# Compression's first layer with the token spans stationary in two column halves, fourteen gate tiles by half-size products, and all token sums on GpSimd

## The chip, the cores and the metric

One core of one Trainium2 chip runs the whole program. The metric is the device time of one execution in microseconds (us); less is better. Engines are named as in the profile: PE (TensorE matmuls), PEld (its weight loads), DVE (VectorE), ACT (ScalarE), POOL (GpSimd), SP (SyncE, which issues the transfers). All data are float32, which the profile records as two PE instructions for each matmul.

## What is computed

A decoder trunk of two equal layers on 512 tokens of 1024 channels. Each layer:

```
h = rmsnorm(x);  z = h @ W_in
q, kc, vc, ks, vs, kw, vw, nsa_g, u, g_a, g_s = split(z)
a = NSA(...)        # compressed + selected blocks + sliding window
s = S5(u)           # grouped complex-diagonal state space, then GLU
x = x + (sigmoid(g_a) * (a @ proj_nsa) + sigmoid(g_s) * (s @ proj_s5)) @ W_out
x = x + HierMoE(rmsnorm(x))     # top-1 group, top-2 of its experts
```

The first layer of the compression, on which the change works, is this; each of the 31 blocks takes 32 tokens of 64 channels, and two neighbours share 16 tokens:

```
def compress(t, pos_emb, w1, w2):           # once for keys, once for values
    blocks = heads(t, Hkv)[:, :, blk_idx] + pos_emb      # 2 heads x 31 blocks x 32 x 64
    flat = blocks.reshape(B, Hkv, n_cmp, CMP_BLOCK * dh)
    return jax.nn.gelu(flat @ w1) @ w2                   # w1: 2048 x 128
```

## The kernel before

**Stages.** A layer runs in three stages: the projections and the mixer's inputs, then attention with the state space, then the experts. PE sets the pace of the first two; in the third the weights of the experts stream through SP's queue (489.25 MB are read from memory in the whole program). The loads of the experts are issued as the arena's places come free of the mixer, so that whatever moves the mixer's end moves the experts. The second layer is the same code and runs the same order.

**The two merge gates as fill.** g_a and g_s make 16 tiles of 128 channels x 512 tokens. They are needed only at the merge, so PE computes them in small pieces between other work, by `fill(cost)` (L918). The unit is one matmul 128x256 wide. `FILL` lists the pieces in order. `PLAIN` pairs of tiles (2 pairs, so 4 tiles) are computed directly, as matmuls 128x512 (L935). The other twelve tiles (`FAST` = 6 pairs) are computed by Strassen-Winograd: seven products of half size for each pair (L916, 128x256), of sums of weights (`weight_sum`, L667, POOL) and sums of tokens (`token_sums`, L1984, DVE: t1 to t4, 128x1024 each). Two products go to the two halves of one bank; ACT copies the bank out (`evac_fill`, L1496) and POOL adds it to the gate tiles (`half_sums`, L634; L632). `ORDER` is the order of the seven products, and `FILL_AHEAD` is the work that is placed ahead of the scores of attention: 80 units.

**Around the first layer of the compression.** PE's order is written out by hand: the transposes tq(t) and tk(t) of the normalised queries and keys (L996, L1001), `hid` (L972), the output steps of the state space `s5y` (L1060, eight steps of 12 matmuls, four of them each on 32 columns of the array), with `cmp` (second layer of the compression, L892) and `tkc` (transpose of the compressed keys, L1004) between them, then the scores (L1074, L1084). In `hid` the weights `w1[:, c, m, :]` (c: keys or values, m: one of 16 token pairs) are stationary, 128 columns, and the tokens `k2` move, 93 columns wide at a stride of 8: 62 blocks of the two heads and 31 columns of the position embedding, whose column gives the bias of the gelu. There are 16 x 2 matmuls, in two banks, and after three of four m a `fill(2)`, 12 in all.

**DVE and POOL there.** DVE normalises queries and keys of tile t in `norm_qk(t)` (L1862 to L1880), runs `chunk_scan` (L1961 to L1982), whose end raises `states_ready` for s5y, and then the four token sums (L1997). `chunk_scan` begins when PE has transposed the last keys, ("tk", 3). POOL fills the position columns of k2 (L625) early, then waits for ("tk", 3), clears two tiles (L628) and makes the first four weight sums (L679) before the sums of the products' results.

**Chunks of weights.** The columns of W_in arrive through four places, numbered by `RING_AT`. A place is loaded again when `last_use` says it was read; the last chunks are those of the projections ahead of the merge.

Of the kernel before, what the change touches and what calls it, by code (L numbers as in the profile page):

```python
# [20 lines left out]
ALU = mybir.AluOpType  # L21
# [3 lines left out]
P = 128  # L25
D = 1024
S = 512
# [44 lines left out]
PLAIN = 2  # L72
FAST = 8 - PLAIN
C_FAST = 5 + PLAIN
RING_AT = [0, 1, 2] + [3, 3] + [3, 2] + [0, 2] * (FAST // 2) + [1, 0, 2]


def chunk_before(c):

    if c == C_FAST + FAST:  # L80
        return c - 2
    return max((i for i in range(c) if RING_AT[i] == RING_AT[c]), default=None)
# [6 lines left out]
GROUPS += [("hid", 0), ("hid", 1), ("cmp", 0), ("cmp", 1), ("tkc", 0)]  # L89
# [7 lines left out]
ORDER = (1, 6, 2, 7, 4, 5, 3)  # L97
PRODUCTS = [(j, n) for j in range(FAST) for n in ORDER]
FILL = [("gate", i) for i in GATES[:2 * PLAIN]] + [("fast", g) for g in range(14)]
for m in range(4):  # L100
    FILL += [("z", m), ("fast", 14 + m)]
FILL += [("fast", g) for g in range(18, len(PRODUCTS) // 2)]
# [4 lines left out]
def fill_cost(g):  # L107

    return 2 * KD if g[0] == "gate" else 4 if g[0] == "z" else KD


FILLED = 2 * PLAIN + 2
# [69 lines left out]
def trunk(nc, a, out):  # L182
    with ExitStack() as ctx:
# [78 lines left out]
        k2 = view(76, 2, KVH + 1, S // 2)  # L262
# [15 lines left out]
        w2 = view(98, 2, DH)  # L278
        us5 = view(110, NST, S5J)
# [14 lines left out]
        rtmp = spare[:, 2 * D:2 * D + 384].rearrange("p (i g d) -> p i g d", i=4, g=12)  # L294
        fast_p = [spare[:, 2432 + S * i:2432 + S * i + S] for i in range(2)]
# [127 lines left out]
        cpos_zero = sem("cpos_zero")  # L423
        cpos_ready = sem("cpos_ready")
        kv_zero = sem("kv_zero")
# [63 lines left out]
        def last_use(c):  # L489

            if c < 3:
                return pj_done, GIDX[("tok", c + 2, NT - 1)] + 1
# [18 lines left out]
        def fast_tokens():  # L511
# [3 lines left out]
                        t1=raw[:, :, 0:256], t2=raw[:, :, 256:512], t3=hT[:, LOW, LATE], t4=t4)  # L515
# [62 lines left out]
        def _(pool):  # L578
# [40 lines left out]
            with pool.Fori(0, DEPTH) as l:  # L619
                for i in range(2):  # L620
                    pool.memset(k2[:, i, KVH, :], 0.0).then_inc(cpos_zero, 1)
                pool.wait_ge(cpos_zero, 2)
                pool.wait_ge(mix_in, N_MIX_IN)
                for i in range(2):
                    pool.tensor_copy(k2[:, i, KVH, 0:CSTR], cpos[:, i, :]).then_inc(cpos_ready, 1)  # L625
                pool.wait_ge(pj_done, GIDX[("tk", NT - 1)] + 1)
                for y in (vcs, kcT):
                    pool.memset(y, 0.0).then_inc(kv_zero, 1)  # L628
# [51 lines left out]

                for n in range(1, 5):
                    weight_sum(0, n)
                for g in range(len(PRODUCTS) // 2):
# [188 lines left out]
        def _(pe):  # L872
# [26 lines left out]
            def fast_product(j, n, k):  # L899
# [6 lines left out]
                elif n == 7 and k == 0:  # L906
                    pe.wait_ge(h_sums, 4)
                    pe.wait_ge(w_sums, 4 * j + 3)
# [4 lines left out]
                dst, w, h = bank[:, FB, HALVES[half]], fast_weights(j)[a][:, k, :], fast_tokens()[b][:, k]  # L913
                if n == 4:
                    dst = dst.rearrange("p (b d) -> p b d", b=2)
                return pe.matmul(dst, w, h, start=(half == 0 and k == 0), stop=(half == 1 and k == KD // 2 - 1))  # L916
# [26 lines left out]
            def group(g, tap=None):  # L943
# [20 lines left out]
                elif kind == "hid":  # L964
# [3 lines left out]
                    pe.wait_ge(cpos_ready, 2)  # L968
                    n = KVH + 1
                    for m in range(CSTR):  # L970
                        for c in range(2):
                            r = pe.matmul(bank[:, (i + c) % NBANK, 0:n * NCMP].rearrange("p (h c) -> p h c", h=n),  # L972
                                          w1[:, c, m, :], k2[:, c, :, m:m + CSTR // 2 * (NCMP - 1) + 1:CSTR // 2],
                                          start=(m == 0), stop=(m == CSTR - 1))
                            if m == CSTR - 1 and c == 0:
                                r.then_inc(pj_done, 1)
                        if m % 4 < 3:
                            fill(2)
# [1345 lines left out]
```

## Time and profile before

| what | value |
|---|---|
| device time, median of 3 | 1830.31 us (1829.23 to 1834.97) |
| the profiled execution | 1832.97 us, span 1831.3 us |
| span of one layer | 907.85 us from L1961 of the first to that of the second |
| PE busy | 1664.1 us, 91% |
| DVE, ACT, POOL busy | 580.3, 411.5, 201.1 us |
| granted TensorE clock, mean | 0.973 of full |

Times inside the program are us from the span's start. The rows below are of the first layer unless they say otherwise.

### The profile page before, as it was taken

Reading aid. Unit: us, or ns where it says so; the run is one execution under the profiler, and the core shown is the slowest. Engines: PE = TensorE matmul, PEld = TensorE weight load, DVE = VectorE, ACT = ScalarE, POOL = GpSimd, SP = SyncE. Lnnn points to the kernel's source line nnn. Section 1 sums busy time; section 2 is a strip of 40 time slices with the busy share of each in tenths; the row PEclk is TensorE's granted clock in tenths of the full one; section 3 lists DMA queues with packets and bytes.
Section 4 is the critical chain, followed back from the end, with each engine's and each line's share of the span. In section 5 each row is a group of like instructions: output and inputs, shape, how many; then the busy total and the mean of one; then the engine's idle time right before and its main releaser. Section 6 shows DMA issues by size and latency. Waiting matters only on the chain. (4 is left out here: it accounts for less than half of the span.)

```text
span 1831.3 us, 22306 instructions
## 1 busy us (share of the span) xinstructions
PE 1664.1 (91%) x7754; PEld 878.8 (48%) x7754; DVE 580.3 (32%) x1686; ACT 411.5 (22%) x1003; POOL 201.1 (11%) x289
## 2 busy tenths in 40 slices
PE   8999999999998778788899999999999987878888
PEld 6667766454443333333377677554544433323333
DVE  4875356334000000000278744563340000000003
ACT  3323555011111111111123254540111111110101
POOL 1012421000100100000000134210001100000000
PEclk9999999999999989999999999999999999998999
DMA  6631101564999999999947111026569999999998
GB/s 171 142 106 47 47 24 47 207 253 177 409 426 428 427 425 426 427 427 428 390 113 195 52 47 47 24 54 237 227 242 412 426 427 427 425 428 427 427 427 345
DMA packets 121906, 496.44 MB, mean 271 GB/s; under 512 B 42036, under 2 KB 78900, under 8 KB 94160
## 3 DMA queue, kind: packets, MB, share of 16 engines
q1 hardware_dynamic: 109584, 472.75, 65.2%
q0 software_dynamic: 8928, 16.52, 2.4%
q10 hardware_dynamic: 3296, 5.84, 0.8%
q8 instruction: 64, 1.05, 0.2%
q14 instruction: 34, 0.28, 0.0%
HBM read 489.25 MB, written 30.47 MB: 284 GB/s over the span
## 5 line engine op out<-in xcount | busy, mean ns | idle before, releaser
L1262 PE MATMUL bank<-arena 128*64 128x512 f32 x2176 | 694.3, 622 | 88.5 <-DMA arena<-in_expert_up 31.3
L1262 PEld LDWEIGHTS bank<-arena 128*64 128x64 f32 x2176 | 229.8, 143 | 352.0 <-issue 351.8
L2224 DVE SCALAR_TENSOR_TENSOR arena<-bank,halves,arena 128x512 f32<-128x512 f32 x32 | 24.0, 751 | 815.0 <-PE bank L1262 815.0
L1262 PE MATMUL bank<-spare_slot,arena 128*64 128x512 f32 x320 | 138.1, 630 | 29.9 <-ACT arena L1664 9.1
L1262 PE MATMUL bank<-h,arena 128*64 128x512 f32 x320 | 140.5, 615 | 26.9 <-DMA arena<-in_expert_gate 11.9
L892 PE MATMUL bank<-arena,hT 128*128 128x256 f32 (+1 forms) x512 | 119.5, 390 | 3.3 <-DMA arena<-in_w_in 2.5
L1262 PE MATMUL bank<-hT,arena 128*64 128x512 f32 x256 | 119.4, 622 | 0.0
L1155 PE MATMUL bank<-arena,hT 128*128 128x512 f32 x256 | 115.0, 597 | 0.0
L892 PEld LDWEIGHTS bank<-arena,hT 128*128 128x128 f32 x512 | 96.7, 192 | 19.9 <-issue 2.7
L1662 ACT ACT_TABLE_LOAD x32 | 41.1, 1283 | 264.8 <-PE bank L1262 264.8
L916 PE MATMUL bank<-hT,arena 128*128 128x256 f32 x384 | 97.0, 387 | 0.0
L1262 PEld LDWEIGHTS bank<-h,arena 128*64 128x64 f32 x320 | 42.1, 141 | 110.3 <-issue 110.3
L1262 PEld LDWEIGHTS bank<-spare_slot,arena 128*64 128x64 f32 x320 | 41.6, 145 | 110.2 <-issue 110.2
L1664 ACT ACTIVATE arena<-bank 128x512 f32<-128x512 f32 x32 | 19.1, 597 | 307.9 <-PE bank L1299 307.9
L1547 ACT ACTIVATE arena<-bank,nbias 128x32 f32<-128x32 f32 (+4 forms) x192 | 83.3, 447 | 6.5 <-DVE nbias L2031 6.4
L892 PE MATMUL bank<-arena 128*128 128x512 f32 (+1 forms) x216 | 84.1, 551 | 0.0
L916 PEld LDWEIGHTS bank<-hT,arena 128*128 128x128 f32 x384 | 68.5, 191 | 14.7 <-issue 7.8
L916 PE MATMUL bank<-h,arena 128*128 128x256 f32 x288 | 72.0, 386 | 0.0
L1155 PEld LDWEIGHTS bank<-arena,hT 128*128 128x128 f32 x256 | 46.6, 190 | 49.4 <-issue 49.4
L2031 DVE TENSOR_REDUCE nbias<-bank 128x1 f32<-128x128 f32 (+3 forms) x128 | 54.8, 483 | 46.2 <-PE bank L1086 46.2
L935 PE MATMUL bank<-hT,arena 128*128 128x512 f32 x128 | 66.5, 601 | 1.0 <-ACT arena L1505 0.9
L679 POOL TENSOR_TENSOR arena<-arena 128x512 f32<-128x512 f32 x48 | 61.5, 1282 | 0.6
(377 smaller groups left out, 1948.5 us busy)
## 6 DMA issues: line engine op xcount, KB each, us to landing
arena<-in_expert_up SPq DMA_DIRECT2D x48, 2048.0 KB, 38.1
arena<-in_expert_gate SPq DMA_DIRECT2D x44, 2048.0 KB, 34.1
arena<-in_expert_down SPq DMA_DIRECT2D x44, 2048.0 KB, 38.9
arena<-in_w_in SPq DMA_DIRECT2D x26, 1024.0 KB, 6.1
spare_slot<-in_expert_gate SPq DMA_DIRECT2D x8, 2048.0 KB
h<-in_expert_gate SPq DMA_DIRECT2D x8, 2048.0 KB
hT<-in_expert_up SPq DMA_DIRECT2D x8, 2048.0 KB, 40.8
spare_slot<-in_expert_down SPq DMA_DIRECT2D x8, 2048.0 KB
```

Of the source, the lines that this page charges most:

```text
L679: pool.tensor_tensor(out=w[out_], in0=w[x1], in1=w[x2], op=op).then_inc(w_sums, 1)
L892: r = pe.matmul(dst, w, m, start=(i == 0), stop=(i == len(pairs) - 1))
L916: return pe.matmul(dst, w, h, start=(half == 0 and k == 0), stop=(half == 1 and k == KD // 2 - 1))
L935: r = pe.matmul(bank[:, FB, :], lhs, rhs, start=(k == 0), stop=(k == n - 1))
L1155: r = pe.matmul(bank[:, c, :], mergedT[:, k, P * t:P * t + P], w_o[:, c, k, :], start=(k == 0), stop=(k == KD - 1))
L1262: r = pe.matmul(dst[CAP * e:CAP * e + CAP, :], moving[:, k, CAP * e:CAP * e + CAP], w, start=(k == 0), stop=(k == n - 1))
L1547: act.activation(p, s, ACT.Exp, scale=-1.0, bias=nbias[:, n % 2, i:i + 1], accum_out=rsum[:, n % 2, i:i + 1])\
L1662: act.activation(hid, bank[:, 2, :], ACT.Silu, scale=slot_root).then_inc(silu_done, 1)
L1664: act.activation(actT.rearrange("p a b -> p (a b)"), bank[:, 6, :], ACT.Copy).then_inc(at_ready, 1)
L2031: dve.tensor_reduce(nbias[:, n % 2, i:i + 1], bank[:, i, 0:nk], AX.X, ALU.min).then_inc(max_ready, 1)
L2224: STT(hid, bank[:, 3, :], slot_root, hid, ALU.mult, ALU.mult).then_inc(act_ready, 1)
```

## The change

Per layer, five things.

1. **Gates.** `PLAIN` 2 to 1 and `FAST` 6 to 7: fourteen tiles by products, two directly. The order of the seven products changes, 49 products make 25 groups (the last with one product), and attention takes 164 units of fill where it took 168. `RING_AT` and `last_use` follow.
2. **First layer of the compression.** The tokens are stationary now: `windows` takes 63 blocks (62, and one of no use between the heads) of k2 at a stride of 8, and w1, 128 columns wide, moves. Keys go to the columns and partitions 0 to 62 of one bank, values to 64 to 126. Ahead of them two matmuls put the position term there: `ones` (64 columns) against `hid_pos`. The output is token by channel, so that after the gelu (one ACT instruction, 128x128) a transpose `th` on PE and a copy on ACT bring it round for `cmp`. A `fill(2)` follows each of the 16 m.
3. **Position term.** `hid_pos` is computed by DVE between `norm_qk(3)` and `chunk_scan`: w1 of each m times the position's value, summed over m, 2 + 30 instructions of 128x128. PE's `hid` waits for all of them (`cpos_ready`).
4. **Token sums.** t3, t2, t4, t1 go from DVE to POOL (t3, t2, t1 with 128x1024, t4 in two halves of 512), with t2 in a place of its own. The first four weight sums come ahead of them and wait for the last token projection, not for ("tk", 3). The sums for the fourth group wait for `states_ready`.
5. **s5y** has its `fill(2)` in four of eight steps only, and `th` stands behind its first step.

```diff
-PLAIN = 2
+PLAIN = 1
-RING_AT = [0, 1, 2] + [3, 3] + [3, 2] + [0, 2] * (FAST // 2) + [1, 0, 2]
+RING_AT = [0, 1, 2] + [3, 3] + [3] + [0, 2] * (FAST // 2) + [0] + [2, 3, 0]
-ORDER = (1, 6, 2, 7, 4, 5, 3)
+ORDER = (1, 2, 6, 7, 4, 5, 3)
...
-FILLED = 2 * PLAIN + 2
+FILLED = 2 * PLAIN + 6
...
+                pool.wait_ge(pj_done, GIDX[("tok", 5, NT - 1)] + 1)
                 for n in range(1, 5):
                     weight_sum(0, n)
-                for g in range(len(PRODUCTS) // 2):
+                b = fast_tokens()
+                halves = lambda y: y.rearrange("p (a k) s -> p a k s", a=2)
+                pool.wait_ge(fill_done, 2 * PLAIN)
+                pool.tensor_tensor(out=b["t3"], in0=b["b22"], in1=b["b12"], op=ALU.subtract).then_inc(h_sums, 1)
+                pool.wait_ge(h_sums, 1)
+                pool.tensor_tensor(out=tok_t2, in0=halves(b["t3"]), in1=halves(b["b11"]), op=ALU.add).then_inc(h_sums, 1)
+                pool.wait_ge(pj_done, GIDX[("tk", NT - 1)] + 1)
...
+                for g in range((len(PRODUCTS) + 1) // 2):
+                    if g == 3:
+                        pool.wait_ge(states_ready, 2)
...
-                    pe.wait_ge(cpos_ready, 2)
-                    n = KVH + 1
+                    pe.wait_ge(ones_ready, 1)
+                    pe.wait_ge(cpos_ready, 2 * CSTR)
+                    for c in range(2):
+                        pe.matmul(b[DH * c:DH * c + DH, 0:P], ones, hid_pos[:, c, :], start=True, stop=False)
+                    n = KVH * (NCMP + 1) - 1
+                    windows = k2.rearrange("p c h t -> p c (h t)")
                     for m in range(CSTR):
                         for c in range(2):
...
+                            r = pe.matmul(b[DH * c:DH * c + n, 0:P],
+                                          windows[:, c, m:m + CSTR // 2 * (n - 1) + 1:CSTR // 2], w1[:, c, m, :],
+                                          start=False, stop=(m == CSTR - 1))
...
+                elif kind == "th":
+                    pe.wait_ge(pj_evac, GIDX[("hid", 0)] + 1)
+                    r = pe.transpose(b[:, 0:P], ghid[:, :], ident[:, :])
...
-                            if part == 0:
+                            if part == 0 and k == 0:
                                 fill(2)
...
                 evac(("hid", 0))
-                evac(("hid", 1))
+                evac_fill(6)
+                evac(("th", 0))
...
-                        TT(b[out_], x1, x2, ALU.subtract).then_inc(h_sums, 1)
-
+                dve.wait_ge(mix_in, N_MIX_IN)
+                for m in range(CSTR):
+                    for i in range(2):
+                        w, c = w1[:, i, m, :], cpos[:, i, m:m + 1]
+                        if m:
+                            dve.wait_ge(cpos_ready, 2 * (m - 1) + i + 1)
+                            r = STT(hid_pos[:, i, :], w, c, hid_pos[:, i, :], ALU.mult, ALU.add)
+                        else:
+                            r = TS(hid_pos[:, i, :], w, c, None, ALU.mult)
+                        r.then_inc(cpos_ready, 1)
                 dve.wait_ge(pj_done, GIDX[("tk", NT - 1)] + 1)
                 chunk_scan()
-                token_sums(1, 2)
-                token_sums(4, 3)
```

The next listings show the order of instructions on an engine, one row for each run of like ones (arena, hT and h are the large buffers; bank is PSUM).

PE at the beginning of the first layer of the compression, before:

```order
L996 MATMUL bank<-ident,arena 128x128 x4
L1001 MATMUL bank<-ident,h 128x128 x2
L935 MATMUL bank<-hT,arena 128x512
L972 MATMUL bank<-arena 128x93 x2
L935 MATMUL bank<-hT,arena 128x512
```

and after, where L938 is the half-size product:

```order
L1023 MATMUL bank<-ident,arena 128x128 x4
L1028 MATMUL bank<-ident,h 128x128 x2
L938 MATMUL bank<-hT,arena 128x256 x2
L993 MATMUL bank<-arena 64x128 x2
L998 MATMUL bank<-arena 63x128 x2
L938 MATMUL bank<-arena 128x256 x2
```

The wide direct gate matmuls are gone from between the pairs, and each pair stands between half-size products; the two position matmuls (L993) lead.

PE at its end, before:

```order
L972 MATMUL bank<-arena 128x93 x2
L1060 MATMUL bank<-arena,spare_slot 32x128 x4
L916 MATMUL bank<-hT,arena 128x256 x2
L1060 MATMUL bank<-arena 32x128 x8
L892 MATMUL bank<-arena 31x64 x6
```

and after:

```order
L998 MATMUL bank<-arena 63x128 x2
L938 MATMUL bank<-arena 128x256 x2
L1087 MATMUL bank<-arena,spare_slot 32x128 x4
L938 MATMUL bank<-hT,arena 128x256 x2
L1087 MATMUL bank<-arena 32x128 x8
L1007 MATMUL bank<-ident,arena 128x128
L1087 MATMUL bank<-arena,spare_slot 32x128 x4
```

One step of s5y stands ahead of the transpose `th` (L1007), and another between it and `cmp`.

POOL ahead of the sums of the results, before (with the semaphores it waits for):

```order
L625 COPY arena<-cpos 128x16
L628 MEMSET arena 128x256 [waits pj_done]
L628 MEMSET arena 128x64
L679 TENSOR_TENSOR arena<-arena 128x512 [waits ring_in0]
L679 TENSOR_TENSOR arena<-arena 128x512 [waits w_sums]
L679 TENSOR_TENSOR arena<-arena 128x4x128
```

and after:

```order
L679 TENSOR_TENSOR arena<-arena 128x512 [waits w_sums]
L687 TENSOR_TENSOR hT<-hT 128x4x256 [waits fill_done]
L689 TENSOR_TENSOR arena<-hT 128x2x512 [waits h_sums]
L695 TENSOR_TENSOR h<-hT,arena 128x2x2x128 [waits h_sums,pj_done]
L697 TENSOR_TENSOR h<-hT,arena 128x4x256
L699 MEMSET arena 128x256
```

DVE in the same place, before:

```order
L1865 TENSOR_TENSOR h<-spare_slot 128x2x2x8
L1866 TENSOR_TENSOR h<-spare_slot 128x2x2x8
L1961 TENSOR_TENSOR arena<-bank,arena 128x1024
L1962 TENSOR_TENSOR arena<-bank,arena 128x1024
L1963 TENSOR_TENSOR arena<-bank,arena 128x1024
```

and after:

```order
L1894 TENSOR_TENSOR h<-spare_slot 128x2x2x8
L1895 TENSOR_TENSOR h<-spare_slot 128x2x2x8
L2021 TENSOR_SCALAR arena<-arena,cpos 128x128 x2
L2019 SCALAR_TENSOR_TENSOR arena<-arena,cpos 128x128 x30
L1990 TENSOR_TENSOR arena<-bank,arena 128x1024
```

The 32 instructions of the position term stand between the last normalisation and the scan on DVE, beside POOL's token sums of five instructions.

## Rows read from the trace of the kernel before

**Rows 1.** The page: the mean GB/s of transfers in 40 equal slices.

```profile
GB/s 171 142 106 47 47 24 47 207 253 177 409 426 428 427 425 426 427 427 428 390 113 195 52 47 47 24 54 237 227 242 412 426 427 427 425 428 427 427 427 345
```

**Rows 2.** Windows: stretch; its length, busy us (instructions) of each engine; clock, DMA.

```profile
130.00:152.30 22.30, 22.21 (x90) 15.27 (x88) 22.04 (x31) 1.64 (x5) 5.26 (x6) 1.00 0.00 1
```

**Rows 3.** Waits of PE from 100 to 330: total us, times, longest.

```profile
PE bank L1114 <- DVE arena L2057: 1.6, 8, 0.2
...
PE bank L935 <- ACT arena L1505: 0.5, 1, 0.5
```

**Rows 4.** Timeline of PE at hid: start, length, instructions (two records a matmul).

```profile
130.73 0.90 PE L972 MATMUL bank<-arena 128*128 128x93 f32 x4
...
132.32 0.84 PE L972 MATMUL bank<-arena 128*128 128x93 f32 x4
132.98 1.04 PE L935 MATMUL bank<-hT,arena 128*128 128x512 f32 x2
...
152.31 0.43 PE L1060 MATMUL bank<-arena,spare_slot 128*32 128x128 f32 x8
```

**Rows 5.** Timeline of PE: half-size products alone, and one matmul pair on 64 columns.

```profile
168.66 3.67 PE L916 MATMUL bank<-h,arena 128*128 128x256 f32 x16
172.26 0.38 PE L1084 MATMUL bank<-arena 64*128 64x128 f32 x2
...
179.55 0.65 PE L1114 MATMUL bank<-arena,h 128*64 128x256 f32 x4
180.13 0.92 PE L916 MATMUL bank<-h,arena 128*128 128x256 f32 x3
```

**Rows 6.** Timeline of PE: one step of s5y with its fill, and the next.

```profile
162.44 0.40 PE L1060 MATMUL bank<-arena,spare_slot 128*32 128x128 f32 x8
162.77 1.13 PE L916 MATMUL bank<-hT,arena 128*128 128x256 f32 x4
163.83 0.64 PE L1060 MATMUL bank<-arena 128*32 128x128 f32 x16
164.29 0.40 PE L1060 MATMUL bank<-arena,spare_slot 128*32 128x128 f32 x8
```

**Rows 7.** Timeline of ACT: second direct gate copied out; table load of hid's gelu.

```profile
124.33 0.60 ACT L1505 ACTIVATE arena<-bank 128x512 f32<-128x512 f32 x1 [5.67 <-PE bank L935]
...
152.42 1.28 ACT L1469 ACT_TABLE_LOAD   x1
```

**Rows 8.** Timeline of DVE: 128x128 pieces; the scan's beginning, idle time ahead in brackets.

```profile
90.72 0.29 DVE L1797 TENSOR_TENSOR arena<-arena,turnv 128x128 f32<-128x128 f32 x1
90.93 0.28 DVE L1798 TENSOR_TENSOR arena<-arena,turnv 128x128 f32<-128x128 f32 x1
...
129.83 1.22 DVE L1961 TENSOR_TENSOR arena<-bank,arena 128x1024 f32<-128x1024 f32 x1 [8.61 <-PE bank L1001]
...
134.48 2.02 DVE L1965 TENSOR_TENSOR arena<-arena 128x1024 f32<-128x1024 f32 x1
136.42 1.21 DVE L1966 TENSOR_TENSOR arena<-arena 128x1024 f32<-128x1024 f32 x1
```

**Rows 9.** Timeline of POOL: weight sums, later one sum of results.

```profile
130.22 5.20 POOL L679 TENSOR_TENSOR arena<-arena 128x512 f32<-128x512 f32 x4
...
247.33 0.76 POOL L632 TENSOR_TENSOR arena<-spare_slot 128x256 f32<-128x256 f32 x1 [5.92 <-ACT spare_slot L1503]
248.05 1.38 POOL L679 TENSOR_TENSOR arena<-arena 128x512 f32<-128x512 f32 x1
```

**Rows 10.** Timeline of DVE: the same four instructions, beside POOL and without it.

```profile
246.76 2.89 DVE L2050 TENSOR_SCALAR arena<-arena,rscale 128x384 f32<-128x384 f32 x4
...
254.24 1.41 DVE L2050 TENSOR_SCALAR arena<-arena,rscale 128x384 f32<-128x384 f32 x4
```

**Rows 11.** Windows around an idle stretch of PE among the experts.

```profile
678.00:680.30 2.30, 0.00 (x0) 0.03 (x1) 0.00 (x0) 0.00 (x0) 0.00 (x0) 0.50 1.04 440
680.30:684.80 4.50, 4.50 (x12) 1.56 (x14) 0.00 (x0) 0.00 (x0) 0.00 (x0) 0.50 0.99 419
```

More of the change, by code:

```diff
@@ L88 @@
 GROUPS += [x for t in range(NT) for x in (("tq", t), ("tk", t))]
-GROUPS += [("hid", 0), ("hid", 1), ("cmp", 0), ("cmp", 1), ("tkc", 0)]
+GROUPS += [("hid", 0), ("th", 0), ("cmp", 0), ("cmp", 1), ("tkc", 0)]
 GIDX = {g: i for i, g in enumerate(GROUPS)}
@@ L278, in trunk @@
         w2 = view(98, 2, DH)
+        ghid = view(98.5, P)
+        hid_pos = view(99, 2, P)
+        ones = view(80, DH)
         us5 = view(110, NST, S5J)
@@ L619, in _ @@
             with pool.Fori(0, DEPTH) as l:
[L620 to L628, printed above, removed]
+                pool.memset(ones, 1.0).then_inc(ones_ready, 1)
                 def add(out_, x1, x2):
@@ L679, in weight_sum @@
                     pool.tensor_tensor(out=w[out_], in0=w[x1], in1=w[x2], op=op).then_inc(w_sums, 1)
+                pool.wait_ge(pj_done, GIDX[("tok", 5, NT - 1)] + 1)
                 for n in range(1, 5):
                     weight_sum(0, n)
-                for g in range(len(PRODUCTS) // 2):
+                b = fast_tokens()
[5 more added lines that the diff above has]
+                pool.wait_ge(pj_done, GIDX[("tk", NT - 1)] + 1)
+                pool.wait_ge(h_sums, 2)
+                for i in range(2):
+                    two = slice(2 * i, 2 * i + 2)
+                    blocks = lambda y: y.rearrange("p k (b d) -> p k b d", b=2)
+                    pool.tensor_tensor(out=b["t4"][:, two], in0=blocks(b["b21"][:, two]), in1=blocks(tok_t2[:, i]),
+                                       op=ALU.subtract).then_inc(h_sums, 1)
+                pool.tensor_tensor(out=halves(b["t1"]), in0=halves(b["b22"]), in1=tok_t2, op=ALU.subtract).then_inc(h_sums, 1)
+                for y in (vcs, kcT):
+                    pool.memset(y, 0.0).then_inc(kv_zero, 1)
+                for g in range((len(PRODUCTS) + 1) // 2):
+                    if g == 3:
+                        pool.wait_ge(states_ready, 2)
                     group_sums(g)
@@ L912, in fast_product @@
                 half = product_at(j, n) % 2
-                dst, w, h = bank[:, FB, HALVES[half]], fast_weights(j)[a][:, k, :], fast_tokens()[b][:, k]
+                dst, w, h = bank[:, FB, HALVES[half]], fast_weights(j)[a][:, k, :], (tok_t2[:, k // 2, k % 2] if b == "t2" else fast_tokens()[b][:, k])
                 if n == 4:
                     dst = dst.rearrange("p (b d) -> p b d", b=2)
-                return pe.matmul(dst, w, h, start=(half == 0 and k == 0), stop=(half == 1 and k == KD // 2 - 1))
+                return pe.matmul(dst, w, h, start=(half == 0 and k == 0), stop=((half == 1 or (j, n) == PRODUCTS[-1]) and k == KD // 2 - 1))
             def fill(cost):
@@ L1383, in _ @@
                 s5_step(("s5y", 0, 1))
+                group(("th", 0))
+                s5_step(("s5y", 1, 2))
                 group(("cmp", 0))
                 group(("cmp", 1))
-                s5_step(("s5y", 1, S5L))
+                s5_step(("s5y", 2, S5L))
                 group(("tkc", 0))
@@ L1618, in _ @@
                     evac(("tk", t))
[L1619 removed]
+                for i in range(2, 6):
                     evac_fill(i)
                 evac(("hid", 0))
[L1622 removed]
+                evac_fill(6)
+                evac(("th", 0))
                 evac(("cmp", 0))
@@ L1625, in _ @@
                 qk_roots(NT)
-                table_of(ACT.Gelu_apprx_tanh, 3)
+                table_of(ACT.Gelu_apprx_tanh, 1)
                 act.wait_ge(states_ready, 2)
-                evac_fill(4)
+                evac_fill(7)
                 gelus(0)
                 evac(("tkc", 0))
-                evac_fill(5)
                 gelus(1)
```

70 lines of the change are left out of this document (30 added, 40 removed).

## The prediction

> **What bounds the kernel now.** I read the mean transfer rate over the 40 slices first: after the first quarter of each layer it stays near 427 GB/s for some ten slices, the experts [rows 1]. The experts take their places in memory as the mixer leaves them, so a microsecond won or lost in the mixer is one at the end, and the second layer repeats the first. Then the window of the first compression layer: PE is busy 22.21 of 22.30 us and so is DVE (22.04), POOL 5.26 [rows 2]. PE's waits over the whole of attention are three groups, 1.6, 1.5 and 0.5 us, two of them shown [rows 3]. So the mixer is PE's own work, and what counts is, per layer: PE time removed, and any place where PE now waits for another engine.
>
> **PE time, per layer.**
>
> *Fill units.* A direct tile costs 16 units, a product 4, and 16 more units belong to the state space's gates: 4 x 16 + 42 x 4 + 16 = 248 before, 2 x 16 + 49 x 4 + 16 = 244 after. A unit is 0.43 us: 16 records, 8 matmuls, lie between 168.66 and 172.26, 3.60 us with one change of shape [rows 5]. So -4 x 0.43 = **-1.7**.
>
> *The first layer itself.* Two matmuls (four records) take 132.98 - 132.32 = 0.66 us [rows 4]; 16 pairs are 10.6, and with the changes between them the 21.58 us from 130.73 to 152.31 [rows 4] less 12 fills of two units (24 x 0.43 = 10.3) leave about 10.9. The new pair exists in no row. Low bound: both halves work side by side, so a pair costs one matmul of 128 columns, half of 0.43, and the two changes of shape to the fill and back: in a step of s5y the fill of 0.86 takes 163.83 - 162.77 = 1.06 [rows 6], so 0.20; together 0.42. High bound: the two 64-column matmuls of 256 columns took 0.58 [rows 5], and 0.20 on top is 0.78, if what fills these 0.58 is not the columns but the loads of two stationary blocks, which are as many here. They stand between fills in both cases; I take the middle, 0.61. The two position matmuls move 128 columns like one pair and have only the change behind them open: 0.5. 16 x 0.61 + 0.5 = 10.3: **-0.6** (bounds -3.7 and +2.1).
>
> *Fill out of s5y.* A step with its fill takes 164.29 - 162.44 = 1.85 [rows 6]. Without it there are 24 records at the 0.46 for 16 that 163.83 to 164.29 show, 0.69. The fill's own 0.86 moves to hid, so each step saves 0.30: four steps **-1.2**.
>
> *Transpose th.* 0.22 (half a unit) and two changes of shape: **+0.4**.
>
> Sum of PE work: **-3.1**. The array's rule of the Trainium skill speaks for more: TensorEngine Tiling (Array Packing), section "Performance Considerations", gives swapping the operands with two column tiles when the moving side is at most 64 wide, twice the work at a time. By it this term would be -4.9 (5.5 + 0.5 for 10.9), not -0.6. Its section "Key Properties" takes part back, since a change of tiling mode drains the engine, and every pair here stands between two such changes.
>
> **The wait for the position term.** Before, DVE is idle for 8.61 us ahead of 129.83 [rows 8]; hid_pos is placed there, and PE can't start hid (130.73 before) until the last of the 32 is done. Alone they would fit: 128x128 pieces start 0.21 us apart (90.72, 90.93) [rows 8], 32 x 0.21 = 6.7, ready at 121.2 + 6.7 = 127.9. But POOL is at work in the same stretch now. What the trace shows of the two together: L1965 adds two inputs from the large buffer while POOL's four weight sums run (130.22 to 135.42) and takes 2.02; L1966 after them, the same size, takes 1.21 [rows 8, 9]. L1961, with one input in PSUM, took 1.22 beside them. And four L2050 take 2.89 beside two POOL instructions (0.76 and 1.38) against 1.41 without [rows 9, 10]. The 1.48 more are the two POOL instructions less one DVE instruction of 0.33 each: (0.76 - 0.33) + (1.38 - 0.33) = 1.48. So DVE gets about one instruction for each of POOL's. The scaled sums of hid_pos have two inputs from the large buffers, as L1965 has.
>
> The Trainium skill states this as an exclusive lock (SBUF — State Buffer, section "Who interferes with whom"): a DVE instruction with two SBUF inputs contends with a GpSimd instruction that reads SBUF, and who issues first keeps the port for the whole instruction. The trace agrees with its 2.02 against 1.21; no row shows it for a scaled sum, and the page names only `tensor_tensor` for it.
>
> Now the schedule. Weight sums (4 x 1.27 or so: 5.20 for four [rows 9]) start when the last token projection is out, near 106, beside norm_qk(2); they push the statistics of tile 3 and so the end of norm_qk(3) from 121.2 to about 122.4. POOL's t3 starts when the second direct gate has been computed, 124.3 [rows 7]; until then DVE does 9 of 32. POOL: 256 elements take about 0.73, 512 1.27, so 1024 about 2.36; t3, t2 to 129.1, a wait for ("tk", 3) until 129.8, then 2 x 1.27 + 2.36 to 135.0. DVE gets one instruction beside each of the five and three in the gap, 17 done at 135; the other 15 take 3.2, last one at 138.2. PE starts hid at about 138.3, not 130.7: **+7.6** (bounds 5.5, if DVE gets two for one, and 9). Queued behind on DVE are the scan's 20.3 us (129.83 to 150.1), which end near 158 and with six to nine POOL sums beside them 160 to 164; PE's hid takes 24.1 with its 16 fills and ends at 162.4. So s5y waits 0 to 1.7 for the states: **+0.4**.
>
> *Clock.* PE idle for 7.6 us. Among the experts PE has no instruction from 678.00 to 680.30, the granted clock there is 0.50, which is 1.2 of 2.4 GHz, and it stays so for another 4.5 us of work [rows 11], worth 2.2. Here, with a longer idle stretch, part of it may pass before work begins: **+1.7** (0.5 to 2.3).
>
> *The chain behind hid.* Gelu waits for its table, 1.28 [rows 7], then th, its copy on ACT, cmp, the key norm, tkc. Before, PE's steps with fill covered it. Now ACT has evac_fill(6) ahead of the copy of th, and that waits for POOL's sums of the fourth group, which start at `states_ready`; and PE has four fills fewer to do in between. ACT's copy and POOL's pair of sums are 0.6 and 1.5, of which one step of s5y (1.85) covers the most. I take **+1.2** for th and **+0.6** for tkc (0 to 3 together).
>
> Costs nothing: the third chunk of the rings (its load ends some 20 us ahead of the merge), the later half-sums (POOL idle more than half of attention), four token sums off DVE (DVE is not waited for there).
>
> **Sum.** -3.1 + 7.6 + 0.4 + 1.7 + 1.8 = +8.4 a layer, +16.8 for two. The profiled execution would take 1832.97 + 16.8 = 1849.8; it stood 2.7 above the median, and against the median of 1830.3 that is **1847**.
>
> **Rivals.** What a measurement can tell from no change is about 0.3%, 5.5 us.
> - *A: scaled sums don't contend.* hid_pos ends at 128.5 and hid starts as before. For it: 8.61 us idle hold 6.7 of work. Against it: 2.02 and 2.89 [rows 8, 10]. -3.1 + 1.8 = -1.3 a layer: 1827.7.
> - *B: as A, and the chain behind hid is hidden too* (s5y steps cover 1.85 each). -3.1 a layer: 1824. This is the case on the other side, faster than before; it decides as soon as the position term is out before 130.7 and th finds its copy ready.
> - *C: DVE keeps the port and POOL waits.* hid_pos is done at 129, t3 and t2 at 134, and PE stands at its first product with t2, 131.7, for 2.3 us: -1.3 + 2.3 = +1.0 a layer: 1832.
> - *D: pairs cost 0.78* with weight loads in the open, the change doesn't bring the side-by-side work it is written for: +2.7 a layer on the forecast: 1852.
> - *E: pairs at 0.34*, half of the present 0.68 (10.9 / 16), with no change of shape felt: 16 x 0.27 = -4.3 a layer on the forecast: 1838. For it: s5y's four-fold tiling has 16 records in 0.46 [rows 6]; against it: the 0.20 of the same rows. It is what the Trainium skill's rule on swapped operands would give.
>
> **How the numbers follow.** Forecast 0.50, A 0.14, B 0.08, C 0.08, D 0.12, E 0.08. Faster by over 0.3% (below 1824.8): B and a third of A, 0.12. Within: the rest of A, C and a little of the forecast's low end, 0.19. Slower: 0.69. The range goes from A's low side, 1826, to the forecast with the high ends of pair and states, 1855; B and the tail above are left out.
>
> **What would show it.** In the profile after: hid's first matmul at 138 with an idle stretch on PE ahead released by DVE; single 128x128 scaled sums on DVE of 1.2 to 2.4 us while POOL's five sums run and 0.29 else; clock 0.50 behind it; a pair of hid 0.6 after a fill; 1.5 between fills. Wrong it would be if hid starts at 131 (A or B), or if PE's first wait is for token sums (C).

## The result

The changed kernel takes 1842.87 us (median of six, 1840.28 to 1846.01), the kernel before 1829.77 (six, 1828.06 to 1834.97): ratio 1.0071, interval 1.0061 to 1.0081. It is slower by 13.1 us, where 16.8 were forecast. The sign and the range held, but the wait that costs most is not the one the forecast was built on.

### The profile page after: what moved, and what is told of

The parts are those of the page before. It is cut to its first block and busy times, and to the rows that moved or that the text cites. A ratio compares the mean times of both kernels' runs of the same rounds, so it can differ in the third digit from the quotient of the medians.

```text
span 1841.4 us, 22540 instructions
## 1 busy us (share of the span) xinstructions
PE 1656.9 (90%) x7812; PEld 875.1 (48%) x7812; DVE 612.9 (33%) x1742; ACT 415.6 (23%) x1007; POOL 259.4 (14%) x315
## 5 line engine op out<-in xcount | busy, mean ns | idle before, releaser
L1289 PE MATMUL bank<-spare_slot,arena 128*64 128x512 f32 x320 | 132.2, 610 | 30.9 <-ACT arena L1693 9.1
L938 PE MATMUL bank<-hT,arena 128*128 128x256 f32 x448 | 114.1, 388 | 1.7 <-ACT spare_slot L1532 1.6
L679 POOL TENSOR_TENSOR arena<-arena 128x512 f32<-128x512 f32 x56 | 73.9, 1321 | 173.7 <-PE bank L911 172.5
L938 PEld LDWEIGHTS bank<-hT,arena 128*128 128x128 f32 x448 | 79.5, 190 | 18.8 <-issue 6.1
L732 POOL COPY slot_tok<-table 128x1 int32 x28 | 5.1, 183 | 499.4 <-DVE arena L2234 499.4
L632 POOL TENSOR_TENSOR arena<-arena,spare_slot 128x256 f32<-128x256 f32 x70 | 51.2, 747 | 133.8 <-ACT spare_slot L1532 119.7
```

The lines of the kernel that those rows point to most:

```text
L632: return pool.tensor_tensor(out=out_, in0=x1, in1=x2, op=ALU.add)
L679: pool.tensor_tensor(out=w[out_], in0=w[x1], in1=w[x2], op=op).then_inc(w_sums, 1)
L1289: r = pe.matmul(dst[CAP * e:CAP * e + CAP, :], moving[:, k, CAP * e:CAP * e + CAP], w, start=(k == 0), stop=(k == n - 1))
```

## The profile after

PE's waits from 100 to 340, changed kernel (columns as in [rows 3]):

```profile
PE bank L938 <- issue: 3.9, 1, 3.9
PE bank L1141 <- DVE arena L2079: 1.6, 8, 0.2
PE bank L1129 <- DVE arena L2072: 1.4, 4, 0.4
PE bank L938 <- ACT spare_slot L1532: 1.1, 4, 0.3
PE bank L1031 <- DVEq L2030: 0.6, 1, 0.6
...
```

The second line is the first of [rows 3]; the third stood before at 1.5 us, in the part of [rows 3] that is not printed. New are the first (3.9 us), the fourth (ACT copies the products' bank) and the fifth (tkc). There is no wait for the position term. "issue" names no releaser; the timelines of PE, DVE and POOL say which it is. PE:

```profile
129.55 0.44 PE L993 MATMUL bank<-arena 128*64 128x128 f32 x4
129.79 0.43 PE L998 MATMUL bank<-arena 128*63 128x128 f32 x4
134.10 1.10 PE L938 MATMUL bank<-arena 128*128 128x256 f32 x4 [3.88 <-issue]
135.13 0.71 PE L998 MATMUL bank<-arena 128*63 128x128 f32 x4
135.77 2.08 PE L938 MATMUL bank<-arena 128*128 128x256 f32 x4
...
144.76 1.13 PE L938 MATMUL bank<-h,arena 128*128 128x256 f32 x4
145.82 0.51 PE L998 MATMUL bank<-arena 128*63 128x128 f32 x4
146.26 1.13 PE L938 MATMUL bank<-h,arena 128*128 128x256 f32 x4
...
159.96 0.43 PE L1087 MATMUL bank<-arena,spare_slot 128*32 128x128 f32 x8
```

DVE, then POOL:

```profile
121.40 7.96 DVE L2019 SCALAR_TENSOR_TENSOR arena<-arena,cpos 128x128 f32<-128x128 f32 x30
129.28 1.21 DVE L1990 TENSOR_TENSOR arena<-bank,arena 128x1024 f32<-128x1024 f32 x1
```

```profile
123.22 8.36 POOL L687 TENSOR_TENSOR hT<-hT 128x1024 f32<-128x1024 f32 x1 [12.60 <-PE bank L957]
131.66 2.35 POOL L689 TENSOR_TENSOR arena<-hT 128x1024 f32<-128x1024 f32 x1
134.15 4.34 POOL L695 TENSOR_TENSOR h<-hT,arena 128x512 f32<-128x512 f32 x2
```

PE begins the position matmuls at 129.55, on time: hid_pos is out at 129.3. It then has nothing to do until 134.10, where the first product that reads t2 begins (L938 from the arena). t2 (L689) ends at 134.01. It is late because t3 (L687) is recorded with 8.36 us, where t2, a sum of the same size, takes 2.35. Reckoned back from its end (131.58 less 2.35), t3 got to work near 129.2, when DVE went over to L1990, which reads PSUM. So DVE's 30 scaled sums did not share with POOL; they kept it out for 6 us, and none of them is longer than 0.35. That it was they who kept it out is what the first two experiments test.

Windows behind the wait, by the columns of [rows 2]:

```profile
134.00:136.00 2.00, 1.90 (x9) 1.23 (x10) 2.00 (x2) 0.00 (x0) 1.86 (x2) 0.77 0.00 0
136.00:138.50 2.50, 2.50 (x9) 1.36 (x9) 2.46 (x2) 0.00 (x0) 2.50 (x3) 0.50 0.00 0
```

The clock is at 0.50 (1.2 of 2.4 GHz) for all of the second window and about 0.46 of the first (0.77 = 1 - 0.5 x 0.46): 3.4 us, in which PE does half the work, worth 1.7.

One number serves for all runs from here on: **the stretch** from the first matmul of s5v (L1045 before) to the first of the scores (L1074), first layer. Before it is 62.0 us, in the changed kernel 67.2; the second layer repeats both within 0.2. Attention, from there to the first matmul behind the merge, is 198.1 and 197.5.

## The experiments

Line numbers are those of each kernel. e1_no_pos and e9_fills_back leave the position term out, e6_one_input leaves out its sum; all others compute everything. The stretches:

| kernel | stretch, us | time, us | ratio to before |
|---|---|---|---|
| before | 62.0 | 1829.8 to 1830.4 | 1 |
| changed | 67.2 | 1842.9 | 1.0071 |
| e1_no_pos | 62.5 | 1828.2 | 0.9989 (0.9979 to 0.9999) |
| e2_chained | 76.0 | 1857.3 | 1.0144 (1.0127 to 1.0161) |
| e3_split | 72.7 | 1851.6 | 1.0117 (1.0100 to 1.0134) |
| e6_one_input | 71.3 | 1848.7 | one run |
| e7_old_hid | 62.4 | 1831.0 | 1.0002 (0.9993 to 1.0011) |
| e8_one_gap | 73.0 | 1853.4 | one run |
| e9_fills_back | 67.6 | 1840.0 | 1.0052 (1.0037 to 1.0067) |
| e10_sums_on_dve | 66.6 | 1841.7 | 1.0062 (1.0047 to 1.0078) |
| e11_pool_awake | 67.4 | 1843.5 | one run |
| e12_old_hid_late_fill | 61.5 | 1828.5 | 0.9991 (0.9982 to 1.0000) |
| e13_fresh_chain | 73.1 | 1851.6 | one run |
| e14_run_in_chain | 68.1 | 1841.0 | one run |

### Without the position term

```diff
-                    pe.wait_ge(cpos_ready, 2 * CSTR)
-                    for c in range(2):
-                        pe.matmul(b[DH * c:DH * c + DH, 0:P], ones, hid_pos[:, c, :], start=True, stop=False)
...
-                dve.wait_ge(mix_in, N_MIX_IN)
-                for m in range(CSTR):
...
```

> The changed kernel without the position term: DVE's 32 instructions of hid_pos and PE's two position matmuls are left out, the rest is unchanged. In the changed kernel POOL's t3 is recorded from 123.22 for 8.36 us and PE waits 3.88 us ahead of its first product with t2. Theory K (DVE's overlapping two-input instructions kept POOL out until 129.2, and t3 itself takes 2.4): t3 takes 2.3 to 2.5, t2 is there by 128, PE has no wait over 0.5 us and no half clock in this layer; 3.9 + 1.3 (clock) + 0.5 (position matmuls) = 5.7 a layer, 1842.9 - 11.4 = 1831.5 us (1828 to 1834). Rival W (t3 is slow in itself, two reads and a write of hT while PE reads hT): t3 takes 8 us again, the wait stays, and only the 0.5 a layer goes: 1842.

t3 on POOL, timeline:

```profile
124.80 2.36 POOL L687 TENSOR_TENSOR hT<-hT 128x1024 f32<-128x1024 f32 x1 [12.60 <-PE bank L957]
127.23 2.36 POOL L689 TENSOR_TENSOR arena<-hT 128x1024 f32<-128x1024 f32 x1
```

Theory K holds: t3 takes 2.36, the wait of 3.9 is gone, the stretch is 4.7 shorter. The time fell by 14.6, three more than expected; the stretches of two layers explain 9.5 of it. In the profiles the rest lies in stages the edit does not touch, whose lengths scatter by 1 to 3 us from profile to profile (from the first expert matmul of the second layer to the end: 475.6 in the changed kernel's, 472.3 here, 474.8 in e11_pool_awake, which is as slow as the changed one). Why the medians differ by more than the stretches too stays open.

### No two of the scaled sums overlap

```diff
-                            dve.wait_ge(cpos_ready, 2 * (m - 1) + i + 1)
+                            dve.wait_ge(cpos_ready, 2 * m + i)
```

> The changed kernel with each of the 32 position instructions waiting for the one right before it, where it waited for the one before that: same work, but no two of them overlap. Theory K (the port stays with DVE because the next instruction is taken up before the last one is out): POOL now gets in between, t3 ends by 128, DVE does one instruction for each of POOL's, hid_pos ends at 136 or later, and PE waits ahead of the position matmuls, 6 us or more: 1846 to 1852. Rival P (DVE goes before POOL whenever it has an instruction, overlapping or not): the chain takes some 32 x 0.33 = 10.6, t3 starts working only behind it near 131.7, t2 is there at 136.4, and PE waits about 2 ahead of the position matmuls and 4 at the product: 1847 too, but with t3 recorded over 10 us. The trace tells them apart.

Wait of PE, and timelines of POOL and DVE:

```profile
PE bank L993 <- DVE arena L2019: 11.9, 1, 11.9
```

```profile
124.62 2.44 POOL L687 TENSOR_TENSOR hT<-hT 128x1024 f32<-128x1024 f32 x1 [12.61 <-PE bank L957]
```

```profile
122.93 19.69 DVE L2019 SCALAR_TENSOR_TENSOR arena<-arena,cpos 128x128 f32<-128x128 f32 x30
```

POOL got in at once, 2.2 us into DVE's work as in the changed kernel: scaled sums that do not overlap do not keep it out, and Rival P falls. The price was missed, 1857.3 for 1846 to 1852: singly, the sums start 0.39 apart, so the 30 need 11.7 and not 9.9, on top of POOL's turns.

### The position term in two halves

```diff
+                    if t == NT - 1:
+                        dve.wait_ge(mix_in, N_MIX_IN)
+                        add_pos(range(CSTR // 2))
...
+                add_pos(range(CSTR // 2, CSTR))
```

The first line stands between qk_mean and the wait for its root.

> The changed kernel with the position term in two halves: 16 of the 32 instructions in DVE's idle 3.25 us between the statistics of the last query tile and their root, the other 16 behind the normalisation as before. Nothing is left out. Theory K: the second half ends near 124.5, POOL's t3 starts then, t2 is there at 129.3, just when PE asks for it (129.8), so PE's wait is 0.5 or less and the clock stays up: 3.9 + 1.3 = 5.2 a layer, 1842.9 - 10.4 = 1832.5 us (1829 to 1835). Rival W (POOL's sums are slow for another reason): t2 stays at 134 and the time at 1843.

DVE's second half, POOL, and PE's waits:

```profile
130.45 8.88 DVE L1865 SCALAR_TENSOR_TENSOR arena<-arena,cpos 128x128 f32<-128x128 f32 x16
```

```profile
131.44 2.54 POOL L695 TENSOR_TENSOR h<-hT,arena 128x512 f32<-128x512 f32 x2 [1.99 <-PE bank L1028]
```

```profile
PE bank L993 <- DVE arena L1865: 7.3, 1, 7.3
...
PE bank L1023 <- DVEq L1926: 1.1, 1, 1.1
```

A miss of 19 us, and the most useful run. The first half pushed the end of norm_qk(3) into the time of t3 and t2. Between its short instructions POOL got in each time (t3 2.41, t2 2.36), and the second half began only at 130.45. Then POOL asked for t4, four instructions into DVE's overlapping chain, and was let in at once. From there DVE got one instruction for each of POOL's, as the prediction had it. So the same two kinds of instruction give either picture.

### Scalings with one input

```diff
-                            r = STT(hid_pos[:, i, :], w, c, hid_pos[:, i, :], ALU.mult, ALU.add)
+                            r = TS(hid_pos[:, i, :], w, c, None, ALU.mult)
```

> The changed kernel with the 30 scaled sums of the position term replaced by scalings with one input tensor (the position term is wrong then: the sum over the 16 pairs is left out). Same number of DVE instructions, same waits. Theory two-input (only a second input from the large buffer takes the port that POOL needs): t3 takes 2.4 from 123.2, no wait of PE at t2: 1832. Rival one-input-too (the four scalings L2050 of the kernel before lost time beside POOL although they have one input tensor): t3 stays blocked until DVE is done at about 129, PE waits 3.9: 1843.

DVE and PE:

```profile
123.00 15.01 DVE L2019 TENSOR_SCALAR arena<-arena,cpos 128x128 f32<-128x128 f32 x30
```

```profile
138.16 0.70 PE L993 MATMUL bank<-arena 128*64 128x128 f32 x4 [7.06 <-DVE arena L2019]
```

Neither theory held. One input contends as well, single pieces taking 2.38 beside POOL, but POOL gets in, and hid starts at 138.16 after 7.06 us: the forecast's picture almost to the number (138.3, 7.6). The 1848.7 was in neither theory. These pieces overlap too (recorded with 0.28, 0.20 apart), so overlap alone does not keep POOL out; it takes the scaled sums as well.

### One gap in the chain

```diff
+                            dve.wait_ge(cpos_ready, 2 * m + i if (m, i) == (6, 0) else 2 * (m - 1) + i + 1)
```

> The changed kernel with one more wait: the 13th of the 32 position instructions on DVE (near 124.2, one us after POOL has asked for t3) waits for the one right before it, so that there is one place where two of them do not overlap. Theory K (overlap keeps the port with DVE): POOL gets in at that place, t3 is recorded with 3.2 to 3.6 us where it had 8.36, DVE's next instruction or two stand for 2.4, and then the overlapping rest keeps t2 out until DVE is done at 131.7: t2 there at 134, PE's wait for t2 3 to 4 us as before, 1843 to 1846. Rival P (a priority of DVE, overlap or not): t3 keeps its 8.4 us.

```profile
124.44 3.12 POOL L687 TENSOR_TENSOR hT<-hT 128x1024 f32<-128x1024 f32 x1 [12.61 <-PE bank L957]
127.65 2.37 POOL L689 TENSOR_TENSOR arena<-hT 128x1024 f32<-128x1024 f32 x1
```

```profile
122.64 16.83 DVE L2019 SCALAR_TENSOR_TENSOR arena<-arena,cpos 128x128 f32<-128x128 f32 x30
```

The gap let POOL in, 3.12 as expected. Expected was too that DVE's rest would shut t2 out again. It did not: t2 followed 0.08 us behind with 2.37, PE waited 8.9 us for hid_pos, and one added wait a layer, which by itself costs 0.1 us, made the program 10 us slower. An exchange once begun went on to POOL's last sum here; that it does so because DVE never gets a chain going again is a reading, not shown.

### Fills as before

```diff
-                        fill(2)
+                        if m % 4 < 3:
+                            fill(2)
...
-                            if part == 0 and k == 0:
+                            if part == 0:
```

> The kernel without the position term (1828.2, 0.9989 of before) with the fills as before the change: 12 of 16 m in the first compression layer and all eight steps of s5y; ACT copies the products' bank behind cmp again. The position term is left out. By the step of the prediction, four fills moved out of s5y save 0.30 each, 1.2 a layer, so undoing it costs +2.4: 1830.6 us. Rival H (fills among the pairs meet the single bank: each of the four groups shows a wait of PE for ACT of 0.24, and s5y's two 0.3 to 0.8): undoing it gives 1 to 2 back: 1827 to 1828.

```profile
PE bank L1085 <- DVE arena L2009: 4.7, 1, 4.7
```

+5.1 us a layer in the stretch, not +1.2. Without the four fills PE is done with hid at 151.4, 4.9 us earlier than in e1_no_pos, and stands 4.7 us for the scan's states, which come at 156.0; the clock is at half for the first 3.8 us of work behind it, another 1.9. The states are later than before (150.1) while POOL's sums run beside the scan, and it is DVE that then bounds the stretch. The step of the prediction (a fill in s5y costs 0.30 more) is right in size, for steps without fill start 0.65 us apart, and was not what these fills are worth.

The run also shows pairs of hid with no fill between them. PE here, then before:

```profile
136.03 0.75 PE L995 MATMUL bank<-arena 128*63 128x128 f32 x8
136.71 1.13 PE L938 MATMUL bank<-hT,arena 128*128 128x256 f32 x4
```

```profile
135.40 1.52 PE L972 MATMUL bank<-arena 128*128 128x93 f32 x8
136.74 1.04 PE L935 MATMUL bank<-hT,arena 128*128 128x512 f32 x2
```

Two pairs take 0.68 here and 1.34 before. A single one takes 0.44 here from its start to the fill's, so the second adds 0.24, where before a pair adds 0.66 to 0.68. So the swap does make a pair short, and what it gains is lost on the changes of shape beside a fill: a fill and a pair in turn take 1.50, which is 0.86 + 0.24 and 0.40 for the two changes.

### t3 and t2 on DVE, position matmuls last

```diff
+                    if m == 5:
...
+                        dve.wait_ge(fill_done, 2 * PLAIN)
+                        TT(b["t3"], b["b22"], b["b12"], ALU.subtract).then_inc(h_sums, 1)
+                        dve.wait_ge(h_sums, 1)
+                        TT(tok_t2, hv(b["t3"]), hv(b["b11"]), ALU.add).then_inc(h_sums, 1)
```

PE's position matmuls stand behind the sixteenth pair.

> The changed kernel with t3 and t2 back on DVE, placed among the position instructions behind the twelfth, and with PE's two position matmuls at the end of the first layer, not ahead of it. Nothing is left out. Theory K: no two-input work of both engines meets ahead of the first product, t2 is there near 127, PE has no wait there and no half clock (-5.2 a layer); DVE's queue is 2.5 us longer, so the scan starts near 131.5 and the states are late by 0 to 2.5: 1842.9 - 10.4 + 2 = 1834 us (1831 to 1837). Rival D (DVE is the bound of this stretch whatever the order): s5y waits for the states by what PE won, 4 or more a layer: 1841.

```profile
PE bank L1083 <- DVE arena L2007: 2.2, 1, 2.2
PE bank L934 <- ACT spare_slot L1528: 2.0, 5, 1.1
```

```profile
130.04 5.39 POOL L691 TENSOR_TENSOR h<-hT,arena 128x512 f32<-128x512 f32 x2 [18.12 <-PE bank L1024]
```

The wait for t2 is gone; 2.2 us for the states and 0.9 more for ACT have come instead, and the clock is at half for 3.4 us behind the first, so Rival D is nearer: 66.6 for 67.2, 1841.7 for its 1841. POOL's first t4 half, asked for nine instructions into DVE's chain, was kept out (5.39 for two). Its place in the cycle of a scaled sum, 0.195 us behind the start of one, is that at which e3_split's t4 got in. So the place in the cycle does not decide.

### What lets POOL in

Three runs on what was open: is it POOL's idle time before, or how long the chain has run?

```diff
-                pool.memset(ones, 1.0).then_inc(ones_ready, 1)
...
                 pool.wait_ge(fill_done, 2 * PLAIN)
+                pool.memset(ones, 1.0).then_inc(ones_ready, 1)
```

> The changed kernel with POOL's small memset of the ones moved from the layer's beginning to right before t3, so that t3 is not POOL's first instruction after 12.6 us of idling. What is open: in the changed kernel (and in the run with one gap) t3 asked in the middle of DVE's chain of overlapping scaled sums and was kept out to its end, as was the first token sum of the run with t3 and t2 on DVE, each POOL's first after 12 to 18 us idle; sums that came to POOL less than 2 us after its last one got in at once, in the middle of the same chain. Theory A (POOL's first instruction after a long idle stretch is the one kept out, an awake POOL finds the 0.05 us between two of DVE's): t3 takes 2.4 to 2.6, hid_pos ends near 139, PE waits 7 to 9 us ahead of the position matmuls, 1850 to 1854. Rival N (who is first keeps the port for the whole chain, whatever POOL did before): t3 takes 8 us, PE waits 3.9 at the first product with t2, 1843.

```profile
124.60 0.15 POOL L686 MEMSET arena<- 128x64 f32 x1 [12.59 <-PE bank L957]
124.71 8.30 POOL L687 TENSOR_TENSOR hT<-hT 128x1024 f32<-128x1024 f32 x1
```

No change: POOL awake is kept out just so. Then, with DVE's chain stopped after six instructions and started anew with POOL's go-ahead:

```diff
+                for q in range(1):
+                    pool.memset(tok_t2, 0.0).then_inc(t2_clear, 1)
...
+                        if (m, i) == (3, 0):
+                            dve.wait_ge(fill_done, 2 * PLAIN)
```

> The changed kernel with DVE's chain of scaled sums stopped after six and started again when POOL's go-ahead for t3 comes (both wait for it), and POOL clearing t2's place once (0.7 us) ahead of t3, so that t3 asks for the port 3 to 4 instructions into a fresh chain. Open is why t3 was kept out in the changed kernel (7 or 8 instructions into the chain, likewise the first token sum of the run with sums on DVE, 8 in) while the run with the split position term let POOL in, 4 instructions into its chain, at the same phase. Theory F (a chain that has just begun can be entered, one that has run in can't): t3 takes 2.4 to 2.6, hid_pos ends after 138, 1848 to 1854. Rival N (the chain that is first keeps the port from its first instruction on): t3 takes over 6 us.

> As the run before, with POOL clearing t2's place three times (2.1 us), so that t3 asks 8 to 9 instructions into the chain. Theory F: t3 is kept out to the chain's end, over 5 us. Rival V (what decides is whether the two have met shortly before, and clearing, which reads nothing, doesn't count): the same answer as in the run before, whichever that is.

POOL in the first of them (one clearing), and in the second (three):

```profile
123.69 0.95 POOL L689 MEMSET arena<- 128x1024 f32 x1 [12.59 <-PE bank L961]
124.72 2.57 POOL L691 TENSOR_TENSOR hT<-hT 128x1024 f32<-128x1024 f32 x1
```

```profile
124.68 2.97 POOL L689 MEMSET arena<- 128x1024 f32 x3 [12.59 <-PE bank L961]
127.73 6.06 POOL L691 TENSOR_TENSOR hT<-hT 128x1024 f32<-128x1024 f32 x1
```

Theory F held both ways and in both layers: asked for 1.06 us into a chain, t3 takes 2.57, hid_pos is late by 9.6 us of PE's time and the kernel takes 1851.6; asked for 3.08 us into it, t3 takes 6.06 and the kernel 1841.0. Rivals N and V fall. All runs with an unbroken chain of scaled sums agree: let in at 0.99 (e3_split) and 1.06 us, kept out at 2.2 (changed), 2.3 (e10_sums_on_dve, e11_pool_awake) and 3.1. Where between 1.06 and 2.2 it turns, and why, stays open. No run tells age from number either: 4 instructions had begun where POOL was let in, 9 to 12 where it was not. Open too is why a chain of one-input scalings let POOL in at 2.2.

### The gates alone

The first layer as before the change (weights stationary, position column, no hid_pos, no th) with all the rest; then with s5y's four fills one step later.

```diff
-                            if part == 0 and k == 0:
+                            if part == 0 and 1 <= S5L * k + i <= S5L:
```

> The gates and token sums of the changed kernel (fourteen tiles by products, sums on POOL, 16 fills among the pairs, four fills fewer in s5y) with the first layer of the compression as it was before: weights stationary, position column in k2, no hid_pos on DVE, no transpose th. Nothing is left out. Theory S (the swap of operands brings nothing by itself, pairs of 0.64 in the trace after against 0.66 before, and what it needs, hid_pos and th, is what costs): like the run without the position term (1828.2) less the transpose and its chain, 0.5 to 1 a layer: 1826.5 us (1825 to 1829), 0.1 to 0.3% faster than before. Rival G (the gates' part costs too, by products' evacuations that PE waits for): 1830 to 1834.

> The gates' part with the old first layer (1.0002 of before, 1.2 us of waiting for ACT at s5y's first fill), with s5y's four fills at steps 1 to 4, not 0 to 3. Nothing is left out. Theory S: the first fill after hid comes 0.65 us later, so the wait falls from 1.2 to 0.5 or less: -0.7 a layer, ratio 0.9995 (0.9985 to 1.0003). Rival R (the first key's chain of the compression now comes earlier against PE and tkc waits instead): ratio 1.0002 to 1.0008.

The first one's wait, which the second doesn't have:

```profile
PE bank L943 <- ACT spare_slot L1530: 1.2, 1, 1.2
```

Theory S on the swap, as the pairs stand here, is borne out by the stretch: 62.4 with the old first layer and 62.5 without position term in the new one. Its time was missed: 1831.0 lies in Rival G's 1830 to 1834, and the 1.2 us for ACT's copy of the products' bank is the kind of wait that G names. So the gates' part alone gained nothing (1.0002). In the second run the later fill gave 0.9 us a layer, and 1828.45 against 1830.2 is the best of the kernels that compute everything; its interval reaches 1.0000, so that it beats the kernel before is likely, not proved.

## Why the prediction was right, and where it was not

- **Direction and range**: right, +13.1 for +16.8, range 1826 to 1855. PE work fell about as forecast, and DVE and POOL meeting in the stretch cost more than that. But by the prediction's own sign ("if PE's first wait is for token sums (C)") its mechanism was wrong, and that its time held is in part luck: the measured case is C, whose price was 1832.
- **The wait**: the step that failed is "DVE gets about one instruction for each of POOL's". It was read from instructions that stand singly or four in a row [rows 8 to 10]. In the changed kernel the chain had run for 2.2 us when POOL asked, and POOL got none: what the prediction had as C, with 0.08. PE waited 3.9 for t2 and not 7.6 for hid_pos. Where POOL did get in, the forecast's picture came: PE waits of 7.1, 7.3, 8.9 and 9.6, times 1848.7 to 1853.4 around its 1847.
- **C's own price**: +1.0 a layer was short of the measured +4.65 mainly because it had 2.3 for the wait and nothing for the clock. Scaled sums start 0.263 apart and not 0.21 [rows 8], so the 32 need 8.4 and not 6.7, and hid_pos and t2 come later for it. (The changed kernel's profile reaches s5v at 104.93, 1.2 us earlier than before. In the prediction's times hid_pos is out at 130.5, not 129, and t2 at 135.2, not 134.)
- **Clock**: 1.7, measured 1.7. The two agree by chance, since the idle stretch was half as long as forecast. Behind the waits of 7 to 10 us it took 3.7 to 5.3 us of work in the first layer, worth 1.9 to 2.6.
- **Pairs**: 0.61 taken, measured 0.24 and 0.40 for the two changes of shape, 0.64. So both halves do work side by side, as the low bound had it (0.22), and the changes cost twice the 0.20 that it took from s5y. All of hid, from 129.55 to 159.96 (30.4 us), less 3.9, 1.7 and 0.7 of waits and clock, is 24.1, the prediction's number. Less 16 fills of 0.86 it is 10.3 for the new layer. The 10.9 of before does not follow from the prediction's subtraction, which leaves 11.3; with the 0.88 that a direct fill of that kernel takes it is 11.0.
- **States**: 0.4 taken, 0 measured, because PE was late itself. The 16 scan instructions took 7.6 us longer beside POOL's sums (lines below), and the states were there at 158.9, only 1.1 before PE came to s5y. So the term was mis-sized for any kernel in which PE is on time: 2.2 in e10_sums_on_dve, 4.7 in e9_fills_back.
- **Chain behind hid**: 1.8 taken. Measured 0.33 (s5y's first fill) + 0.56 (tkc), and three waits of 0.25 for the products' bank, which the prediction had not: 1.6. The table load of the gelu did not count; ACT had it done at 155.6, before hid's end.
- **Fill units**: -1.7 taken, -0.55 measured. Attention lost eight 256-wide records (304 to 296, 1.7 us), but was only 0.55 shorter; the 1.1 between was not traced.
- **Sum by layer**: in the stretch -1.4 + 7.6 + 0.4 + 1.7 + 1.8 = +10.1 was said. Measured are 3.9 + 0 + 1.7 + 1.6 and +5.2 in all (67.2 - 62.0), which leaves -2.0 for PE's work. With attention (-0.55) it is +4.65, where +8.4 was said. Twice that is 9.3; the profiled spans differ by 10.1 and the medians by 13.1. The profile of before was itself 3.2 above its median and that of the changed kernel 0.6, so single profiles can't place the rest, which stays open.

The scan on DVE, before and in the changed kernel:

```profile
137.67 5.16 DVE L1970 TENSOR_TENSOR_SCAN arena<-decay,arena 128x128 f32<-128x128 f32 x16
```

```profile
137.39 12.77 DVE L1999 TENSOR_TENSOR_SCAN arena<-decay,arena 128x128 f32<-128x128 f32 x16
```

The Trainium skill's rule on swapped operands (TensorEngine Tiling (Array Packing), section "Performance Considerations") is to swap and use two column tiles where the moving side is at most 64 wide (here 62 blocks). For pairs that stand together the trace agrees that this pays, 0.24 against 0.66 to 0.68. Between fills of another shape 0.64 against 0.66 shows nothing of it. The exclusive lock of the Trainium skill (SBUF — State Buffer, section "Who interferes with whom") holds here for scaled sums too, in either engine's favour (8.36 us for POOL's 2.36; 2.38 us and more for DVE's 0.35). But that page of the Trainium skill tells of one instruction, and here a chain kept it from one to the next for 6 us.

## What to carry to other kernels

Work moved into an engine's idle gap has to be weighed with what another engine does there that contends with it: 8.4 us fitted into 8.6 idle us, and cost 5 to 11 a layer (stretches of 67.2 and 73.1 against 62.5). If two engines must share, look at who asks first and how long the other has been running without a gap; a single added wait can turn the order round for the whole stretch. Before splitting fills elsewhere, ask whether they are cover for another engine's result. And a matmul made short by using parts of the array wants neighbours of its own shape: 0.40 of changes ate the 0.42 that the swap won in each pair.

## What the hardware showed that was not expected

- Overlapping scaled sums of 128x128 (start to start 0.263 us, each recorded with 0.34) on DVE keep a POOL tensor sum out to their end, if they have run for 2.2 us or more (8.36, 8.30 and 6.06 us for an instruction of 2.36). If the chain is 1.0 us old, POOL gets in within 0.2 us (e3_split, e13_fresh_chain), and then DVE gets one instruction for each of POOL's.
- Scalings with one input of 128x128 contend with POOL as well (2.38 us for 0.28), but never kept it out here.
- A pair of 63-column matmuls in two column halves adds 0.24 us behind another such pair, and 0.64 between matmuls on all 128 columns.
- The 16 scan instructions of 128x128 on DVE (`TENSOR_TENSOR_SCAN`) took 12.77 us beside POOL's sums, 5.16 with POOL idle.
- After 3.9 us without a matmul the clock went to half for 3.4 us, beginning 1.0 us after work had begun again.
